# Decay stage of a two-block kernel: rows spread by one product of 64 high and low rows, and one token tile's gap made by VectorE

## What is computed

```
gap[s, t]      = relu(row[t] + minus_col[s])            # s: key token, t: query token
weighted[s, t] = (k[s] . q[t]) * weight[s] * exp(-gap[s, t]),  kept where s <= t (or s >= t, backward)
out[t]         = sum over s of weighted[s, t] * v[s]
```

## Time and profile before

| what | value |
|---|---|
| median of three runs | 2537.66 us (2535.87 to 2540.64) |
| the profiled execution | 2538.27 us, of which the span is 2536.3 us |
| decay stage, first layer | from 232.1 to 314.9 us of the span |
| decay stage, second layer | from 800.5 to 883.2 us of the span |
| PE, DVE, ACT, POOL busy over the span | 93, 69, 52, 23% |

### The profile page before, as it was taken

The page is one execution under the profiler, slowest core; times in us unless marked ns, Lnnn a source line. Parts: engine busy times, 40 slices in busy tenths (PEclk is TensorE's granted clock), DMA queues, the critical chain, the costliest instruction groups (busy, mean ns, idle before and its releaser), DMA issues. The chain is left out here.

```text
span 2536.3 us, 37032 instructions
## 1 busy us (share of the span) xinstructions
PE 2363.4 (93%) x14184; PEld 1975.0 (78%) x14184; DVE 1755.2 (69%) x2775; ACT 1322.4 (52%) x2660; POOL 594.9 (23%) x333
## 2 busy tenths in 40 slices
PE   8999988988999988978998899999999989999999
PEld 8866776767866766767786689998887866899987
DVE  1846757873856767867698679994257986799942
ACT  3457616763457617755746654443167476444431
POOL 3401305772401205762350010000034400100000
PEclk9999988998999988998998999999999989999999
DMA  4210029983200019982220213322231202133221
GB/s 164 89 34 18 4 83 354 356 309 114 88 34 18 16 61 356 360 293 106 79 87 1 78 54 103 115 99 93 70 110 67 84 1 92 35 121 111 100 83 67
DMA packets 54990, 285.80 MB, mean 113 GB/s; under 512 B 13216, under 2 KB 13216, under 8 KB 28704
## 3 DMA queue, kind: packets, MB, share of 16 engines
q1 hardware_dynamic: 45600, 266.65, 29.3%
q0 software_dynamic: 9216, 16.80, 1.7%
HBM read 275.02 MB, written 25.17 MB: 118 GB/s over the span
## 5 line engine op out<-in xcount | busy, mean ns | idle before, releaser
L253 POOL TENSOR_TENSOR weights_lo<-weights_raw,weights_hi 128x2048 fp32r<-128x2048 f32 (+4 forms) x49 | 221.3, 4516 | 677.9 <-POOLq L120 356.3
L264 PE MATMUL ps<-x_operands,weights_hi 128*128 128x256 f32 x1232 | 349.3, 284 | 7.4 <-DVE weights_lo L2054 6.8
L265 PE MATMUL ps<-x_operands,weights_hi 128*128 128x256 f32 x1232 | 347.0, 282 | 0.0
L266 PE MATMUL ps<-x_operands,weights_lo 128*128 128x256 f32 x1232 | 347.0, 282 | 0.0
L215 ACT ACTIVATE weights_hi<-weights_raw 128x2048 fp32r<-128x2048 f32 (+4 forms) x80 | 136.8, 1709 | 302.3 <-PE ps L266 287.6
L264 PEld LDWEIGHTS ps<-x_operands,weights_hi 128*128 128x128 f32 x1232 | 231.3, 188 | 10.1 <-DVE weights_lo L2054 9.8
L266 PEld LDWEIGHTS ps<-x_operands,weights_lo 128*128 128x128 f32 x1232 | 232.3, 189 | 0.0
L265 PEld LDWEIGHTS ps<-x_operands,weights_hi 128*128 128x128 f32 x1232 | 232.3, 189 | 0.0
L264 PE MATMUL ps<-weights_hi,attn_ht_hi 128*128 128x512 f32 (+2 forms) x576 | 203.6, 353 | 3.7 <-DVE weights_lo L253 2.2
L265 PE MATMUL ps<-weights_lo,attn_ht_hi 128*128 128x512 f32 (+2 forms) x576 | 200.3, 348 | 0.0
L266 PE MATMUL ps<-weights_hi,attn_ht_lo 128*128 128x512 f32 (+2 forms) x576 | 199.5, 346 | 0.0
(11 more groups left out here) (529 smaller groups left out, 6281.2 us busy)
## 6 DMA issues: line engine op xcount, KB each, us to landing
weights_raw<-in_stream SPq DMA_DIRECT2D x96, 1024.0 KB, 4.8
weights_raw<-in_expert_gu SPq DMA_DIRECT2D x34, 1024.0 KB, 9.4
expert_raw<-in_expert_gu SPq DMA_DIRECT2D x30, 1024.0 KB, 9.5
expert_raw<-in_expert_down SPq DMA_DIRECT2D x18, 1024.0 KB, 8.5
weights_raw<-in_expert_down SPq DMA_DIRECT2D x14, 1024.0 KB, 8.3
weights_raw<-in_stream SPq DMA_DIRECT2D x12, 960.0 KB, 4.7
ffn_raw<-in_stream SPq DMA_DIRECT2D x10, 1024.0 KB, 5.0
weights_raw<-in_stream SPq DMA_DIRECT2D x8, 700.0 KB, 8.5
```

Source lines behind the costliest of these rows:

```text
L253: eng.tensor_tensor(lo[:, 0:n], self.env.raw[:, u % self.RAW, 0:n], hi[:, 0:n].bitcast(F32), ALU.subtract).then_inc(self.lo_ready, 1)
L264: nc.tensor.matmul(out, a[0], b[0], start=start, stop=False, **more)
L265: nc.tensor.matmul(out, a[0], b[1], start=False, stop=False, **more)
L266: return nc.tensor.matmul(out, a[1], b[0], start=False, stop=stop, **more)
```

## The change

Rows. At the stage's start DVE writes `picks` (64 x 32, fp32r, two identities of 32 above one another) and `twice` (`cols` beside itself, 64 columns a token tile). PE transposes `twice` into 64 rows of 512 tokens in bank 6; ACT copies all 64 rows into the fp32r tile `rows` (the high parts), and DVE overwrites the lower 32 rows with the original minus the high part (the low parts). From then on the row of a unit is one fp32r matmul of 512 columns: the stationary operand is column k of `picks` repeated 128 times, which picks high row k and low row k, and the moving operand is `rows`. The first two products of unit 0 are issued before the first row, the other two behind the row of unit 1.

Gaps. In each of the eight SSD units ACT makes three of the four gaps, and DVE makes the fourth (key tile 2 of a forward unit, key tile 1 of a backward one, 256 columns either way) with one `tensor_scalar` (add, then max with 0) out of the same PSUM bank, once ACT's three are through (`make_side_gap`). On DVE it stands between the weighting of unit i-1 and the store of unit i-2. Exponential, weighting and masking of that tile come last in their units. Where the unit behind has such a tile, the products of a new group wait for its whole weighting and not tile by tile. The mLSTM units keep their four gaps on ACT.

The core of the diff (semaphore names, and lines that only rename, are left out):

```diff
+    NR = 32
...
+    side = [(1 if u["back"] else 2) if u["group"][0] == "s" else None for u in units]
+    sides = [sum(x is not None for x in side[:i + 1]) for i in range(N)]
+    gaps = [T * (i + 1) - sides[i] for i in range(N)]
+
+    def gap_read(eng, i):
+        eng.wait_ge(gap_ready, gaps[i])
+        if sides[i]:
+            eng.wait_ge(side_gap, sides[i])
...
+        twice = local.enter_context(nc.sbuf_tensor("decay_cols_twice", [P, T, 2 * NR], F32, allow_name_mangling=True))
+        rows = local.enter_context(nc.sbuf_tensor("decay_rows", [2 * NR, S], F32R, allow_name_mangling=True))
+        picks = local.enter_context(nc.sbuf_tensor("decay_picks", [2 * NR, NR], F32R, allow_name_mangling=True))
+        turned = ps[0:2 * NR, 6, :]
...
+                def products(u, each, behind):
+                    for s in each:
+                        if behind is not None:
+                            pe.wait_ge(weighted, T * (behind + 1) if side[behind] else T * behind + s + 1)
+                        nc.tensor.matmul(ps[:, s, :].rearrange("p (t c) -> p t c", t=T), u["k"][:, s, :],
+                                         u["q"], start=True, stop=True).then_inc(products_ready, 1)
+
+                pe.wait_ge(cols_then_rows_lo, 1)
+                for t in range(T):
+                    last = nc.tensor.transpose(turned[:, t * P:(t + 1) * P], twice[:, t, :], ident)
+                last.then_inc(row_ready, 1)
+                products(units[0], range(2), None)
+                pe.wait_ge(cols_then_rows_lo, 3)
                 for i in range(N + 2):
                     if i < N:
                         if i >= 2:
-                            pe.wait_ge(gap_ready, T * (i - 1))
-                        for t in range(T):
-                            r = cols[:, t, units[i]["row"]:units[i]["row"] + 1].to_broadcast([P, P])
-                            last = nc.tensor.matmul(ps[:, 4 + i % 2, t * P:(t + 1) * P], r, ident, start=True, stop=True)
-                        last.then_inc(row_ready, 1)
-                    if 1 <= i <= N and new_group[i - 1]:
-                        u = units[i - 1]
-                        for s in range(T):
-                            if i > 1:
-                                pe.wait_ge(weighted, T * (i - 2) + s + 1)
-                            last = nc.tensor.matmul(ps[:, s, :].rearrange("p (t c) -> p t c", t=T), u["k"][:, s, :],
-                                                    u["q"], start=True, stop=True)
-                            last.then_inc(products_ready, 1)
+                            gap_read(pe, i - 2)
+                        k = units[i]["row"]
+                        nc.tensor.matmul(ps[:, 4 + i % 2, :], picks[:, k:k + 1].to_broadcast([2 * NR, P]), rows[:, :],
+                                         start=True, stop=True).then_inc(row_ready, 1)
+                    if i == 1:
+                        products(units[0], range(2, T), None)
+                    elif 1 < i <= N and new_group[i - 1]:
+                        products(units[i - 1], range(T), i - 2)
                     if i >= 2:
                         j = i - 2
                         u = units[j]
                         if j == N - 1:
-                            pe.wait_ge(gap_ready, T * (N - 1))
+                            gap_read(pe, N - 2)
                             sums.half(pe, 0, 2, 0)
...
-                pe.wait_ge(gap_ready, T * N)
+                gap_read(pe, N - 1)
...
-                nc.vector.tensor_scalar(minus_cols[:, :, :], cols[:, :, :], -1.0, None, ALU.mult).then_inc(negated, 1)
+                nc.vector.tensor_tensor(picks[:, :], ident[0:2 * NR, 0:NR], ident[0:2 * NR, NR:2 * NR], ALU.add)
+                nc.vector.tensor_copy(twice[:, :, :].rearrange("p t (u c) -> p t u c", u=2),
+                                      cols[:, :, :].unsqueeze(2).to_broadcast([P, T, 2, NR])).then_inc(cols_then_rows_lo, 1)
+                nc.vector.tensor_scalar(minus_cols[:, :, :], cols[:, :, :], -1.0, None, ALU.mult).then_inc(cols_then_rows_lo, 1)
+                dve.wait_ge(rows_hi_then_floors, 1)
+                nc.vector.tensor_tensor(rows[NR:2 * NR, :], turned[NR:2 * NR, :], rows[NR:2 * NR, :].bitcast(F32),
+                                        ALU.subtract).then_inc(cols_then_rows_lo, 1)
                 for t in range(2):
                     last = values.copy(nc.vector.tensor_copy, t)
                 last.then_inc(values_ready, 1)
+                def make_side_gap(i):
+                    if i < N and side[i]:
+                        s = side[i]
+                        a, b = span(units[i], s)
+                        col = units[i]["col"]
+                        dve.wait_ge(gap_ready, gaps[i])
+                        if i >= 2:
+                            dve.wait_ge(weighted, T * (i - 1))
+                        nc.vector.tensor_scalar(gap[:, i % 2, s, a:b], ps[:, 4 + i % 2, a:b], minus_cols[:, s, col:col + 1], 0.0,
+                                                ALU.add, ALU.max).then_inc(side_gap, 1)
+
+                dve.wait_ge(cols_then_rows_lo, 3)
+                make_side_gap(0)
                 for i in range(1, N + 2):
...
-                        for s in range(T):
+                        own = [x for x in range(T) if x != side[j]]
+                        for n, s in enumerate(own + ([side[j]] if side[j] else [])):
                             a, b = span(u, s)
                             dve.wait_ge(products_ready, T * (groups - 1) + s + 1)
-                            dve.wait_ge(exp_done, T * j + s + 1)
+                            dve.wait_ge(exp_done, T * j + n + 1)
                             nc.vector.scalar_tensor_tensor(out=wq[:, j % 2, s, a:b], in0=ps[:, s, a:b],
                                                            scalar=u["weight"](s), in1=gap[:, j % 2, s, a:b],
                                                            op0=ALU.mult, op1=ALU.mult).then_inc(weighted, 1)
+                    make_side_gap(i)
...
-                act.wait_ge(negated, 1)
+                act.wait_ge(row_ready, 1)
+                nc.scalar.activation(rows[:, :], turned, ACT.Copy).then_inc(rows_hi_then_floors, 1)
+                act.wait_ge(cols_then_rows_lo, 2)
                 for i in range(N):
-                    act.wait_ge(row_ready, i + 1)
+                    act.wait_ge(row_ready, i + 2)
                     if i == 2:
-                        nc.scalar.activation(cols[:, :, 16:24], cols[:, :, 16:24], ACT.Exp, scale=-1.0).then_inc(floors_made, 1)
+                        nc.scalar.activation(cols[:, :, 16:24], cols[:, :, 16:24], ACT.Exp, scale=-1.0).then_inc(rows_hi_then_floors, 1)
                         values.copy(lambda out, x: nc.scalar.activation(out, x, ACT.Copy), 3).then_inc(values_ready, 1)
                     if i >= 2:
                         act.wait_ge(weighted, T * (i - 1))
-                    for s in range(T):
+                    for s in (x for x in range(T) if x != side[i]):
                         a, b = span(units[i], s)
                         col = units[i]["col"]
                         nc.scalar.activation(gap[:, i % 2, s, a:b], ps[:, 4 + i % 2, a:b], ACT.Relu,
                                              bias=minus_cols[:, s, col:col + 1]).then_inc(gap_ready, 1)
-                    for s in range(T):
+                    own = [x for x in range(T) if x != side[i]]
+                    for s in own + ([side[i]] if side[i] else []):
                         a, b = span(units[i], s)
-                        act.wait_ge(gap_ready, T * i + s + 1)
+                        if s == side[i]:
+                            act.wait_ge(side_gap, sides[i])
+                        else:
+                            act.wait_ge(gap_ready, gaps[i] - len(own) + own.index(s) + 1)
                         nc.scalar.activation(gap[:, i % 2, s, a:b], gap[:, i % 2, s, a:b], ACT.Exp, scale=-1.0
                                              ).then_inc(exp_done, 1)
...
-                    for s in range(T):
-                        pool.wait_ge(weighted, T * i + s + 1)
+                    own = [x for x in range(T) if x != side[i]]
+                    for n, s in enumerate(own + ([side[i]] if side[i] else [])):
+                        pool.wait_ge(weighted, T * i + n + 1)
                         d = wq[:, i % 2, s, s * P:(s + 1) * P]
```

More of the change, by code:

```diff
@@ L1250, in decay_stage @@
     names = ("products_ready", "row_ready", "gap_ready", "exp_done", "weighted", "masked", "out_ready",
-             "out_stored", "negated", "floors_made", "values_ready", "vector_step")
-    (products_ready, row_ready, gap_ready, exp_done, weighted, masked, out_ready, out_stored, negated, floors_made,
-     values_ready, step) = (env.sem("decay", n) for n in names)
+             "out_stored", "cols_then_rows_lo", "rows_hi_then_floors", "values_ready", "side_gap", "vector_step")
```

(7 more changed lines are left out.)

## The result

The changed kernel takes **2548.61 us** (median of 6 executions, 2545.22 to 2554.51) against 2536.26 us for the kernel before (6 executions, 2535.02 to 2540.64). The ratio is 1.0048, with a 95% interval of 1.0034 to 1.0061: slower by 12.35 us, where the prediction had 8.7 faster.

A forecast was written before the change was run, and what follows sets the result against it. PE, busy 93% of the span, was taken as the bound, with DVE becoming slowest in SSD units. Gains of 1.1 (SSD) and 3.4 (mLSTM) made 4.5 a layer, 9.0 in two: 2537.7 to 2529 us, range 2524.5 to 2533.

The forecast's parts named there:

- the 4 in 100: Chance left for other outcomes, among them that the stage doesn't hand its gain on.
- Row product, 0.24: PE's new row matmul takes 0.24 us, saving 0.70 a unit, 11.2 in 16 units.
- DVE's round of 2.88: SSD units: DVE becomes slowest at 2.88 us, against ACT 2.77 and PE 2.43; a steady unit gains 0.25.
- rival B: PE stays the bound and its saving arrives but for the start: 9.6 us a layer, 2518.5; chance 0.10.
- The SSD half: Stage's first half, up to the products of unit 8: gains 1.1 us a layer.
- ACT's and DVE's gap: SSD units: the gap taken off ACT is worth 0.36 to 0.50 us; on DVE it costs 0.45.
- Rival C: SSD rounds: the ACT-DVE hand-off costs 0.5 us in six rounds, a layer gains 1.5, 2534.7; chance 0.22.
- The start: Stage's start: row preparation makes ACT's first gap begin 2.2 us later, mostly won back by unit 4's products.
- The mLSTM half, 3.4: Stage's second half: PE gives 1.40 us a pair, 4.2 less 0.8 for a late mask, so 3.4 a layer.
- the mask step: mLSTM half: POOL's mask of unit 12, behind DVE's weighting, comes late for PE's outputs; 0.8 us lost.
- The tail: Stage's end, DVE's own work: doesn't shrink, moves earlier as a whole.
- Rival D: The row is priced as float32, 0.90 us, and a layer loses 1.9: 2541.5; chance 0.06.

The follow-up runs named there:

- e2: Changed kernel with the row by four float32 matmuls as before, leaving only DVE's gap: 2537.70 us, 1.0012 of the kernel before.
- e12: Changed kernel plus ten idle PE matmuls ahead of unit 0's outputs alone: 2541.02 us, 1.0019 of the kernel before.
- e5: Kernel before plus three idle DVE additions ahead of unit 0's weighting, making PE wait: 2552.21 us, 1.0040 of the kernel before.
- e9: Changed kernel plus idle PE matmuls at the start and ahead of outputs of units 0, 2, 12 and 14: 2532.25 us, 0.9986 of the kernel before.
- e10: e6 with all gaps on ACT: 2526.69 us, 0.9968 of the kernel before.
- e6: e4 plus idle PE matmuls ahead of outputs of units 0, 12 and 14: 2527.31 us, 0.9962 of the kernel before.
- e11: Changed kernel plus three idle PE matmuls at the stage's start alone: 2550.02 us, 1.0053 of the kernel before.
- e4: Changed kernel with float32 rows kept for units 0 and 1, the new rows prepared behind them: 2531.94 us, 0.9984 of the kernel before.
- e3: Changed kernel plus idle PE matmuls, three at the start and ten ahead of unit 0's outputs: 2540.93 us, 1.0021 of the kernel before.
- e1: Changed kernel with all gaps back on ACT, the row product kept: 2550.66 us, 1.0063 of the kernel before.
- e8: e4 with all gaps on ACT: 2537.10 us, 0.9996 of the kernel before.

## Why the prediction was wrong

**The step that failed** is in the first paragraph: "the clock granted is 1.00, the full one". It was read as a property of the stage, and it held only as long as PE hardly paused in it (e2, with one pause of 0.50 a layer, kept it). The prediction then made PE pause: at the start for DVE's doubled columns, with a first gap 2.2 late, and "PE pauses of some tenths before outputs". Each was charged its own length at most, and the start's was even declared won back; the pause ahead of unit 0's outputs has no term at all. In the runs the fall behind that pause of 2.1 cost at least 5.4 a layer (changed kernel against e12), a fall behind a pause of 2.2 in the kernel before 8.1 (e5), and the fall at the start 1.6 up to the first gap (e12's two layers). The trace of the kernel before had shown that the clock can fall: outside the stage it was 0.50 from 361.1 to 398.6, where PE was busy for 17.9 of 37.5 us. No rival had the clock in it; it sat unnamed in the 4 in 100.

Against 78.6 forecast for a layer the account is: 89.3 measured, less 5.4 with unit 0's outputs filled (e12: 83.6 and 84.2), less 4.5 for the other stretches and their pauses (e9: 79.4), which leaves 0.8.

**Row product, 0.24: too small.** The records in the changed kernel, where the clock is full:

```profile
264.81 0.49 PE L1301 MATMUL ps<-decay_rows,decay_picks 64*128 64x512 f32 x1
...
265.23 2.44 PE L1321 MATMUL ps<-proj,decay_weighted 128*128 128x64 f32 x20
...
267.60 0.49 PE L1301 MATMUL ps<-decay_rows,decay_picks 64*128 64x512 f32 x1
...
273.29 0.50 PE L1301 MATMUL ps<-decay_rows,decay_picks 64*128 64x512 f32 x1
...
273.63 3.59 PE L1287 MATMUL ps<-proj 64*128 64x512 f32 x8
...
282.32 0.50 PE L1301 MATMUL ps<-decay_rows,decay_picks 64*128 64x512 f32 x1
...
282.33 3.70 PE L1287 MATMUL ps<-proj 64*128 64x512 f32 x8
```

From row to outputs 0.42, and from outputs to the next row 2.37 where it was 2.18: together the row costs 0.6, not 0.24, and PE's SSD round is 2.79 instead of 2.43. The pitch of the earlier trace rows was read among fp32r neighbours; this row stands alone between float32 matmuls. So a unit saves about 0.34 where outputs follow. The error hardly moved the sum, for the sum went by DVE's round of 2.88: at full clock PE's round is 2.80 to 2.89 (outputs at 252.98, 255.78 and 258.67 in e9) and DVE's 2.85 without a pause (gaps at 254.97 and 257.82). That PE sets the round as soon as DVE's gap is gone (e10, 2.80 again) is rival B's order of engines, but not its gain.

**The SSD half** of e9 gains 0.2 (32.07 from 229.31 to 261.38) instead of 1.1. Of the 0.9 that are missing 0.6 lie ahead of unit 4's products, which begin 17.44 behind the stage's start where the forecast had 16.84, and 0.3 behind them. No run splits this further.

**ACT's and DVE's gap.** DVE's took 478 ns (eight of them, by form) against 0.45, right. Its worth was wrong: ACT's relief isn't needed, and e10 is as fast as e6. Rival C isn't borne out: e2 loses 0.1 a stage at PE's old round, and at the new one e6, with the hand-off, is level with e10, without it.

**The start.** The first gap begins 5.20 behind the stage's start (237.91 less 232.71), forecast 3.44 (235.55 less 232.11): the two products ahead of the row take 3.50 at half clock instead of 1.8. At full clock it is 3.55 to 3.59 (e12's first layer, e9, e11), so this term was right but for the clock. The larger cost of the late first gap comes at unit 0's outputs.

**The mLSTM half, 3.4: right in the sum** (3.47), by luck in part, for two errors cancel. From row to row (273.29, 282.32, 291.13 and 300.38) the three pairs take 9.03, 8.81 and 9.25, forecast 8.67 where PE sets them. And the mask step, 0.8 by forecast ahead of unit 12's outputs, was a pause of 0.14 there; the larger one, 0.59, came ahead of unit 14's, behind the end of this half. The row costs 0.34 ahead of products on partitions 0 to 63 and only 0.01 ahead of those on 64 to 127 (282.32 and 282.33; the rows show 64 partitions, which ones stands in the kernel). From the row to the outputs behind the products that is 3.86 (291.13 to 294.99) against 3.63 (282.32 to 285.95), so 0.23 of the row's price comes back.

**The tail: fixed only at full clock.** It grew by 1.07, with the third stretch at half clock behind that pause: PE's filler ends last, at 321.75, DVE at 320.94. In e9, without the stretch, it is 14.50 (294.25 to 308.75), as before.

**Rival D** had the sign by another mechanism: the row isn't priced as float32 (0.42, not 0.90), and its total of 2541.5 is no support for it.

**What stays open:** what decides whether a pause makes the clock fall. 2.2 did in one layer of e5 and not in the other, 0.97 likewise in e4, 0.50 did in both layers of e3 and never in e2's profile. Counted over the profiled layers, a fall began by 1.6 us behind their end for 7 of 8 pauses of 2.1 to 2.7 ahead of unit 0's outputs (changed kernel, e1, e5, e11), by 0.6 us for 5 of 6 of 2.4 at the start (changed kernel, e1, e12) and by 2.4 us for 13 of 16 of 0.6 ahead of unit 14's outputs. Yet the 1.69 for which PE stands still at the barrier ahead of the stage was followed by none within 8 us in 22 of 22 layers (kernel before, e2 to e11). So the length of a pause alone doesn't decide. e4's range, 2524.68 to 2538.64, mixes cases: its three executions at a granted clock of 0.967 took 2524.7 to 2527.3, its five at 0.963 took 2535.4 to 2538.6. Not tried: a start in which ACT or POOL prepares the rows while the stage before still runs.

## What to carry to other kernels

Where PE is full and its clock reads 1.00, a change that opens a pause of even half a microsecond on it can cost many times the pause: look at the granted clock around every new wait first, and give PE idle matmuls there (here 20 a layer were worth 9.9 us in the profiled executions, 8.2 by the medians). Prices of a matmul taken from a run of its own kind don't hold between another kind; read the distance to both neighbours. Compare two versions only once both keep the clock: the gap on DVE looked useful (e4 against e8) until then (e6 against e10). A pause can also make no fall in the one execution that is profiled, so compare the granted clock of several.

## What the runs showed of the hardware

- In the decay stage the granted clock stood at 0.50 in stretches of 3.4, 6.8, 17.1 and once 20.5 us, and PE was busy in nearly all of that time (16.80 of 16.80 us from 244.6 to 261.4 in the changed kernel, 18.00 of 18.00 around the one in e5).
- In three executions the same pause, among the same instructions, was followed by a fall in one layer only (e5: 84.9 and 93.1; e4: 78.8 and 86.7; e12 at the start: first gap 3.55 and 5.18 behind it).
- A 64-row fp32r product on partitions 0 to 63 and float32 products on partitions 64 to 127 start 0.01 us apart, against 0.34 where both use the lower rows. The Trainium skill (TensorE: Matmul & The Clock Gate, Packing small matmuls) has matmuls on different row groups run concurrently; the trace agrees, for two unrelated products that nobody paired.
